# A convolution taken by blocks of two feature tiles, and an output sum moved behind the next decay matrix

## What is computed

```python
z, xbc, dt = jnp.split(u, [SSD_WIDTH, SSD_WIDTH + SSD_CONV_DIM], axis=-1)
xbc = jax.nn.silu(causal_depthwise_conv(xbc, conv_w, conv_b))
xs, bm, cm = jnp.split(xbc, [SSD_WIDTH, SSD_WIDTH + G * N], axis=-1)
...
seg = cs[..., :, None] - cs[..., None, :]
lmat = jnp.where(causal, jnp.exp(jnp.where(causal, seg, 0.0)), 0.0)
y_diag = jnp.einsum('bcgls,bcgels,bcsgep->bclgep', cb, lmat, xdt)
y_off = jnp.einsum('bclgn,bcgepn,bcgel->bclgep', cm, start_states, jnp.exp(cs))
y = y_diag + y_off + xs * d_skip.astype(f32).reshape(G, E, 1)
y = y.reshape(bsz, seq, SSD_WIDTH) * jax.nn.silu(z.astype(f32))
```

## Time and profile before

| what | value |
|---|---|
| median of 3 runs | 2740.55 us (2740.46 to 2740.57) |
| the profiled execution | 2743.45 us, of which its span 2742.2 us |
| mean granted TensorE clock | 0.997 of full speed |
| TensorE busy with matmuls | 2711.7 us, 99% |
| VectorE, ScalarE, GpSimd busy | 62%, 48%, 3% |
| read from HBM | 501.87 MB, 184 GB/s over the span |

### The profile page before, as it was taken

The page is one execution under the profiler, slowest core; times in us unless marked ns, Lnnn a source line. Parts: engine busy times, 40 slices in busy tenths (PEclk is TensorE's granted clock), DMA queues, the critical chain, the costliest instruction groups (busy, mean ns, idle before and its releaser), DMA issues.

```text
span 2742.2 us, 39458 instructions
## 1 busy us (share of the span) xinstructions
PE 2711.7 (99%) x16390; PEld 2323.9 (85%) x16390; DVE 1699.7 (62%) x1979; ACT 1307.8 (48%) x1672; POOL 88.8 (3%) x109
## 2 busy tenths in 40 slices
PE   9999999999999999999999999999999999999998
PEld 8887778888988888888888888888888888888887
DVE  7787677645655555556555656556666656665675
ACT  6744536444454434434344546445554434443444
POOL 1034000000000000000000000000000000000001
PEclk9999999999999999999999999999999999999999
DMA  7554456555555656556565555555555555555554
GB/s 251 173 187 139 154 171 232 183 199 172 167 171 185 198 188 195 186 187 195 197 189 187 177 189 188 181 167 171 184 174 186 194 199 184 186 198 195 189 185 138
DMA packets 392128, 506.59 MB, mean 185 GB/s; under 512 B 8312, under 2 KB 284496, under 8 KB 391440
## 3 DMA queue, kind: packets, MB, share of 16 engines
q1 hardware_dynamic: 377856, 487.80, 54.7%
q10 hardware_dynamic: 14096, 16.27, 1.9%
HBM read 501.87 MB, written 2.17 MB: 184 GB/s over the span
## 4 chain that ended last, share of the span: by engine, by line
PE 93%; DVE 3%; POOL 2%; ACT 1%; issue 1%; DMA 0%; ACTq 0%; DVEq 0%; POOLq 0%
PE PS L687 40%; PE PS L718 31%; PE PS L715 16%; PE PS L956 1%; POOL slab L3125 1%; POOL slab L3122 1%; DVE wlo L2224 1%; PE PS L758 1%; PE PS L1194 0%; PE PS L1214 0%; ACT whi L1533 0%; PE PS L741 0%; PE PS L1163 0%; PE PS L894 0%; DVE slab L2356 0%
## 5 line engine op out<-in xcount | busy, mean ns | idle before, releaser
L2224 DVE TENSOR_TENSOR wlo<-raw,whi 128x1024 fp32r<-128x1024 f32 x922 | 1126.7, 1231 | 885.3 <-ACT whi L1533 882.1
L1533 ACT ACTIVATE whi<-raw 128x1024 fp32r<-128x1024 f32 x922 | 961.6, 1056 | 1115.0 <-PE PS L715 647.9
L718 PE MATMUL PS<-XX,whi 128*128 128x512 f32 (+1 forms) x3856 | 925.8, 392 | 1.3 <-ACT whi L1533 1.2
L718 PEld LDWEIGHTS PS<-XX,whi 128*128 128x128 f32 (+1 forms) x3856 | 710.6, 189 | 142.7 <-ACT whi L1533 2.3
L687 PE MATMUL PS<-whi,act 128*128 128x512 f32 x2208 | 593.2, 390 | 0.0
L715 PEld LDWEIGHTS PS<-XX,wlo 128*128 128x128 f32 (+1 forms) x3856 | 492.9, 191 | 25.5 <-DVE wlo L2224 7.0
L715 PE MATMUL PS<-XX,wlo 128*128 128x256 f32 (+1 forms) x3856 | 503.0, 283 | 5.6 <-DVE wlo L2224 5.6
L687 PEld LDWEIGHTS PS<-whi,act 128*128 128x128 f32 x2208 | 411.9, 188 | 83.8
L687 PE MATMUL PS<-wlo,act 128*128 128x512 f32 x1104 | 340.1, 389 | 0.0
L687 PE MATMUL PS<-whi,XX 128*128 128x512 f32 x1024 | 279.1, 394 | 0.2 <-issue 0.2
L687 PEld LDWEIGHTS PS<-wlo,act 128*128 128x128 f32 x1104 | 207.2, 188 | 43.6
(11 more groups left out here) (407 smaller groups left out, 1300.2 us busy)
## 6 DMA issues: line engine op xcount, KB each, us to landing
raw<-in_ffn_w SPq DMA_DIRECT2D x128, 1024.0 KB, 5.2
raw<-in_w_in SPq DMA_DIRECT2D x101, 1024.0 KB, 5.1
raw<-in_w_ffn_gate SPq DMA_DIRECT2D x44, 1024.0 KB, 4.9
raw<-in_w_ffn_up SPq DMA_DIRECT2D x44, 1024.0 KB, 4.9
raw<-in_w_ffn_down SPq DMA_DIRECT2D x44, 1024.0 KB, 5.0
raw<-in_w_out SPq DMA_DIRECT2D x32, 1024.0 KB, 5.1
raw<-in_xattn_wk SPq DMA_DIRECT2D x16, 1024.0 KB, 5.2
raw<-in_xattn_wv SPq DMA_DIRECT2D x16, 1024.0 KB, 4.9
```

The costliest lines, as they stand in the source:

```text
L718: mm = T.matmul(ps[0:wd, f, :], k.whi[:, h % 4, o:o + wd], b.x[:, kk, :], start=kk == 0, stop=stop, skip_group_check=True)
L1533: S.activation(k.whi[:, h % 4, 0:b.size], k.raw[:, t % 4, u * b.size:(u + 1) * b.size], ACT.Copy).then_inc(k.w_hi, 1)
L2224: V.tensor_tensor(k.wlo[:, h % 4, 0:b.size], k.raw[:, h // 2 % 4, u * b.size:(u + 1) * b.size], k.whi[:, h % 4, 0:b.size].bitcast(F32), AL ...
```

## The change

Two things. First, every `xbc` block starts its own convolution, over its two feature tiles: two first taps, six tap operations, a SiLU over two tiles. The steps (`yield`) of an evacuation stay as many, and the wait before the matrix engine transposes the convolved tiles goes from the third SiLU to the sixth, which is the same place. Second, VectorE's output sum of a pair (now the inner function `summed`) stands behind D and L of the next pair's first step instead of ahead of them; the last sum stays where it was. The names of the semaphore's values follow the new order. `SSD_DVE` and the other tables are unchanged, and the steps that they count are as many as before.

```diff
@@ names of VectorE's semaphore in the scan
-                (f" D{n + 1}" if n < 7 else "") + f" L{n}" + (f" yg{n // 2}" if n % 2 else "") for n in range(8))
+                (f" D{n + 1}" if n < 7 else "") + f" L{n}" + (f" yg{n // 2 - 1}" if n % 2 == 0 and n else "") for n in range(8)) + " yg3"
@@ ssd_pe
-    T.wait_ge(*k.xbc.ACT("s", 2))
+    T.wait_ge(*k.xbc.ACT("s", 5))
@@ ScalarStream.evacuation
-                S.wait_ge(*k.xbc.DVE("a", j - 1))
+                S.wait_ge(*k.xbc.DVE("a", 2 * j - 2 + b.s))
...
-        if b.kind == "xbc" and b.s:
+        if b.kind == "xbc":
             yield
-            k.wait_both(S, b)
-            o = k.XBC[:, 4 * j:4 * j + 4, :]
-            for f in range(4):
-                at = 4 * j + f
-                ins = S.activation(o[:, f, :], k.buf3[:, f, 0:SEQ], ACT.Identity, scale=k.col["ssd_conv_w"][:, at:at + 1],
-                                   bias=k.col["ssd_conv_b"][:, at:at + 1])
+            S.wait_ge(*k.out_of_psum(b))
+            f0 = 4 * j + 2 * b.s
+            o = k.XBC[:, f0:f0 + 2, :]
+            for f in range(2):
+                at = f0 + f
+                ins = S.activation(o[:, f, :], k.buf3[:, 2 * b.s + f, 0:SEQ], ACT.Identity,
+                                   scale=k.col["ssd_conv_w"][:, at:at + 1], bias=k.col["ssd_conv_b"][:, at:at + 1])
             ins.then_inc(k.xbc.act, 1)
             for _ in range(6):
                 yield
-            S.wait_ge(*k.xbc.DVE("a", j))
+            S.wait_ge(*k.xbc.DVE("a", 2 * j + b.s))
             S.activation(o, o, ACT.Silu).then_inc(k.xbc.act, 1)
@@ VectorStream.evacuation
-        elif b.kind == "xbc" and b.s:
-            k.wait_both(V, b)
-            cw, f0 = k.col["ssd_conv_w"], 4 * j
+        elif b.kind == "xbc":
+            V.wait_ge(*k.out_of_psum(b))
+            cw, f0 = k.col["ssd_conv_w"], 4 * j + 2 * b.s
...
-            V.wait_ge(*k.xbc.ACT("t", j))
-            yield from convolved(k, k.buf3, taps, None, k.XBC[:, f0:f0 + 4, :], k.xbc.dve)
+            V.wait_ge(*k.xbc.ACT("t", 2 * j + b.s))
+            yield from convolved(k, k.buf3[:, two, :], taps, None, k.XBC[:, f0:f0 + 2, :], k.xbc.dve)
@@ convolved
-        for f in range(4):
+        for f in range(dst.shape[1]):
@@ ssd_dve
+    def summed(n):
+
+        c, g, q = ssd_group(n)
+        yg = k.y[:, c, g * 512:g * 512 + 512]
+        V.wait_ge(*sd.PE(f"y{n}"))
+        V.wait_ge(*sd.POOL(f"y{c}"))
+        ins = V.tensor_tensor(yg, yg, PS[:, 6, :], ALU.add)
+        if c > 0:
+            k.dve(ins)
+            k.dve(V.tensor_tensor(hv(k.ssd_junk), hv(PS[:, 7, :]), k.bc(ecs[:, c, 8 * g:8 * g + 8], 64),
+                                  ALU.mult))
+            yield
+            ins = V.tensor_tensor(yg, yg, k.ssd_junk, ALU.add)
+        if g == 0:
+            k.dve(ins)
+            V.wait_ge(*k.out_of_psum(k.blocks_of("tok")[0]))
+            ins = V.tensor_tensor(yg, yg, k.Z[:, c, 0:512], ALU.mult)
+        ins.then_inc(sd.dve, 1)
+        V.wait_ge(*sd.DVE(f"yg{n // 2}"))
+        yield
...
-        if q == 1:
...
+        if q == 0 and n:
+            yield from summed(n - 1)
+    yield from summed(7)
```

## The result

| kernel | median us | runs | lowest to highest |
|---|---|---|---|
| before | 2741.81 | 20 | 2739.81 to 2746.60 |
| after | 2747.03 | 20 | 2744.55 to 2748.52 |

The ratio is 1.0016, 95% interval 1.0009 to 1.0023: by it the change costs 4.4 us (2.5 to 6.3). The two medians of the table are 5.2 us apart, which lies in the same interval. The forecast was +1.7 us, a time of 2742.3, and 2747.03 is within 0.2% of it. The range ended at 2747, so the median stands on its upper edge, 0.03 us past the number as written; counted from the base of the forecast, 2740.55 times 1.0016, the time is 2744.9, inside it. The loss is under the 0.2% I had named as the limit of what can be told, and is nonetheless clear of zero.

What follows compares the result with a forecast made beforehand. TensorE, busy 99%, was taken as the bound, so only its stops in the convolution's stretch and the scan counted. -3.0 + 4.7 = +1.7 us on the median 2740.55 gave 2742.3 us, range 2737.5 to 2747.

Steps and rivals of the forecast that it cites:

- Part one: Projection, convolution started by blocks: gains 3.0 us, first token block at 261.7 instead of 264.75.
- The four rings: Projection: a loop through ScalarE and VectorE once per block, 11.2 us with GpSimd quiet, 14.2 while it solves.
- W(L+7): High weight half on ScalarE, L being a block's last half; said to wait behind the SiLU, two such halves 0.98 each.
- w(L+6): Low weight half on VectorE, L being a block's last half; queued after the last 2 taps, 1.17 us each when quiet.
- The term -3.0: Projection: the gain from convolution by blocks, said to be only the slow clock that the old stops brought.
- Rival (c): Projection: the convolution's split does nothing, one kind of stop replacing the other; 0 + 4.7, 2745.2 us, chance 0.15.
- Part two: Scan, output sums behind the next decay matrix: costs 0.9 + 2.7 + 1.1 = 4.7 us, all on the path.
- rival (b): Lower clock returns behind projection's tiny products (gain 0), slow products follow the scan's longer standstill (6.0): 2746.6 us, chance 0.15.
- the rule with six taps: Projection: shared-port lock; six more taps at 0.42 each could end GpSimd 2.5 us later, but the trace spoke against it.

Runs made afterwards that it cites:

- first taps late: Convolution by blocks only, with ScalarE's two first taps behind the high weight half L+4 instead of ahead of it, against before: ratio 0.9972, 7.7 us less.
- both late: Convolution by blocks only, first taps behind high half L+4 and SiLU behind high half L+7, against before: ratio 0.9972, median 2735.00 us.
- part one alone: Convolution by blocks only, output sums left in their old place, against before: ratio 0.9997, 0.8 us less.
- part two alone: Kernel before with only the output sums moved behind the next D and L, against before: ratio 1.0017, 4.7 us more.

## Why the prediction was right, and where it wasn't

- **The time came out on the upper edge of the range, the sign leaned right, the size was short.** +1.7 was forecast, +4.4 measured.
- **Part one, the mechanism: right.** The four rings were to end at 214.9, 229.0, 242.8 and 257.9; the high halves were ready at 215.3, 229.3, 242.1 and 257.2. Stops of 1.2, 2.2, 2.6 and 1.8 us were forecast, 1.52, 1.95, none and 1.29 came; in the third ring TensorE was late itself, since it had run slowly behind the second. First token block 261.7 forecast, 261.20 measured. Cutting the ring at one link removed all these stops. One reading was short: the stops behind 217.46 are 5.6 us (with 0.52 before 221.80 and 0.42 before 250.10), not 5.2; no term hangs on it.
- **Part one, a link that isn't the only one.** The SiLU (0.63 us, not 0.55) and W(L+7) were in the ring by my text; taking the SiLU out changed nothing, since w(L+6) on VectorE takes as long. That the ring's length came out right all the same is luck: the two ways take equally long.
- **Part one, its value: here the sum failed.** The term -3.0 is the distance to the first token block of one execution, 264.75, and I carried it to the median as if each execution had it. Before has a second level, with A at 64.7 and the first token block 3 us earlier. Against the upper level of A part one gains 3.6 us, against the lower it loses 1.2; measured alone it gives -0.8 (-3.3 to +1.6). I had written that these 3 us were "only the slow clock that the old stops brought", and didn't ask whether it comes every time, though I had noted that this execution was 2.9 us above the median. With -0.8 in place of -3.0 the same sum is +3.9, inside the interval of what was measured. Rival (c), "does nothing in the end", had +4.7, near it, and for part one its zero is inside what was measured.
- **Part two: right in its sum, close in its terms.** From the first token block the third, fifth and seventh pair products start 0.8, 3.3 and 4.8 us later than in before, so the three sums cost 0.8, 2.5 and 1.5; forecast 0.9, 2.7 and 1.1. VectorE waits 2.26 and 4.35 us for the transfers of D3 and D5, as listed. The clock did fall below 0.78 behind the long stop (0.50), rival (b)'s condition, but the price is small: the product took 1.12 us instead of 0.91, and from it to the sixth pair product it is 3.80 us instead of 3.62, not the 1.3 us more of that rival's 6.0.
- **GpSimd: right for a reason I had only half.** It ended no later: 232.63 instead of 234.31. Six executions of before's code end between 233.05 and 234.57, and four with part one between 231.1 and 232.6.
- **Not in the prediction: section C.** It is 28.3 to 30.4 us with no relation to an edit that I can see (before itself: 28.61, 28.39, 30.26). After's 30.43 is the highest, so part of its profiled span is this. The start of A varies by 2.6 us as well.
- **The base.** The three times of before that I had stand at 2740.55; with 17 more, 20 in all, the median is 2741.81. That is 1.3 of the 4.7 us between 2742.3 and 2747.03.

## What to carry to other kernels

When a step of a helper engine is cut into smaller pieces, look for the link by which each piece waits for the other engine ahead of the next weight tile: one `yield` in the right place (first taps behind the tile, not ahead of it) made the same idea worth 7.7 us instead of 0.8. If the way round has a second branch that takes as long, moving a piece off the first gains nothing. An operation may be put behind another only if that other's input is already there; a decay matrix whose transfer is bound to a buffer slot isn't, and the sum it displaced had filled just that wait. And before a term is read off one profiled execution, see whether the stretch repeats: where a clock that falls after a stop is part of it, one execution says what can happen, and further ones whether it always does. The spread of the times is a weak sign: 7 us for before in one set (29 runs), 2 with the first taps late (7 runs), but 4.2 with both late (11 runs), which has no more stops in A; so the expectation that ties the small spread to the missing stops isn't borne out.

## What the hardware showed that I had not expected

**GpSimd and VectorE hold each other up by kind of instruction.** GpSimd's small operations in after, then VectorE's beside them:
```profile
229.15 0.33 POOL L3128 TENSOR_TENSOR slab<-slab 128x84 f32<-128x84 f32 x1
229.55 1.33 POOL L3131 TENSOR_TENSOR slab<-slab 128x84 f32<-128x84 f32 x1
230.97 0.35 POOL L3128 TENSOR_TENSOR slab<-slab 128x58 f32<-128x58 f32 x1
```
```profile
229.45 1.23 DVE L2225 TENSOR_TENSOR wlo<-raw,whi 128x1024 fp32r<-128x1024 f32 x1 [2.17 <-ACT whi L1533]
230.59 1.92 DVE L2357 SCALAR_TENSOR_TENSOR slab<-slab,param_cols 128x256 f32<-128x256 f32 x4
```
An operation of 84 elements takes 0.33 us, and 1.33 when VectorE's subtraction of 1.23 us starts 0.1 us ahead of it; beside the taps one of 58 elements takes 0.35. The short taps, on the other hand, are the ones that grow (0.48 each here, 0.77 where GpSimd's operations are long). By the Trainium skill, "SBUF — State Buffer", section "🔬 SBUF: two separate sides", an operation of VectorE with two inputs in SBUF contends with a GpSimd operation that reads SBUF: whichever of the two starts first has the shared ports for its whole instruction and the other is blocked. The 1.33 agrees. The taps, which have two such inputs too, do not: in before eight of them run in 6.14 us from 214.07, and from 214.75 GpSimd runs eight operations back to back in 5.9 us, 0.64 to 0.74 each, as beside an idle VectorE; both are over after 6.6 us, where one after the other they would take 8.7 (an estimate, 8 times 0.42 and 8 times 0.67). What I had missed in costing the rule with six taps: what holds GpSimd up for long in these rows are the subtractions, and the change adds none of those.

**Clock.** A stop of 1.95 us in after is followed by eight products in 3.17 instead of 2.11 us (granted clock 0.66 in 230 to 235), those of 1.52 and 1.29 by no slow ones. In part one alone 2.17 us are followed by 3.55, in its second execution 2.16 by 2.56. The length of a stop doesn't decide: 2.69 us are followed by a pair in 3.82 in one execution and in 5.34 in another (above). Where a whole stretch of 5 us is slow (255 to 260 in before, 330 to 335 in after) the granted clock is 0.50, half of the chip's 2.4 GHz.

**Stops without a cause in the trace.** Among the tiny products ahead of A TensorE stands for 1.96 to 2.70 us, at the same place in all fourteen executions, and waits for nothing that the profile shows. In ten of them the pair behind the stop is slow, as in part one alone (5.49 us, not 3.82):
```profile
177.70 0.28 PE L985 MATMUL PS<-slab 64*32 64x32 f32 x12 [2.70 <-issue]
177.91 5.49 PE L718 MATMUL PS<-XX,whi 128*128 128x512 f32 x16
```
In four it isn't (3.92 to 3.96 us: before, its third execution, after, part two alone), and these are the four in which A starts at 195.1 to 195.3; in the others it starts at 196.6 to 197.7. The length of the stop doesn't decide here either: 1.96 us are followed by a slow pair, 2.26 by a fast one. Where these stops come from, and what section C does, stays open.
